# Where eighteen expert-weight slots lie, and when the first fourteen of them may be loaded

## The chip, the cores and the metric

One core of a Trainium2 chip runs the whole program. It has a matrix engine (TensorE, PE in the profile), a vector engine (VectorE, DVE), a scalar engine (ScalarE, ACT), GpSimd (POOL), a queue engine (SyncE, SP) and 16 DMA engines that all queues share. The metric is the device time of one execution in microseconds, the median of several runs.

## The reference

One layer of an encoder trunk on 512 tokens of width 1024, in float32: a token mixer (stick-breaking attention and retention, merged by gates), a cross-attention into 256 memory rows, and a mixture of 32 experts of which each token takes four. After it a final RMSNorm. What the change touches is the seam between the last dense product (`@ w_co`) and the experts:

```python
x = x + memory_cross_attention(rmsnorm(x, g_xattn[l]), rmsnorm(mem, g_mem[l]), w_cq[l], w_ckv[l], w_co[l])
x = x + moe_ffn(rmsnorm(x, g_moe[l]), w_router[l], b_router[l], w_exp_in[l], b_exp_in[l], w_exp_out[l], b_exp_out[l])
...
def expert_block(args):
    xb, e = args
    hc = xb @ w1[e] + b1[e]
    glu = jnp.minimum(hc[..., :D_FF], SWIGLU_LIMIT)
    lin = jnp.clip(hc[..., D_FF:], -SWIGLU_LIMIT, SWIGLU_LIMIT)
    act = glu * jax.nn.sigmoid(SWIGLU_ALPHA * glu) * (lin + 1.0)
    return act @ w2[e] + b2[e]
```

Each expert's `w1` is 1024 x 2048 and its `w2` is 1024 x 1024 values: 12 MB for one expert, 384 MB for all.

## The kernel before

**The dense half.** Twenty-seven slabs of weights (`SLABS`), 52 chunks of 1 MB in all (`DENSE`), go through four `raw` buffers. ScalarE copies each half chunk (a piece, 104 in all, `DP`) into a rounded high part `wh` (`split`, L743), VectorE subtracts to get the low part `wl` (`split`, L1090), and TensorE makes each product of three matmuls (`three`, L1665 to L1667). `wh` and `wl` have six places each; a split of piece g waits until TensorE has used piece g-6. The semaphore `w_lo` counts low parts made, `w_used` counts pieces (and later expert chunks) that TensorE has used. The last slabs are `mv1`, `cq0`, `cq1`, then after the cross-attention `co0` (pieces 96 to 99) and `co1` (100 to 103).

**The expert half.** An expert is 12 chunks of 1 MB: 8 of `w_exp_in`, which `up` uses at L1985, and 4 of `w_exp_out`, which `down` uses at L2009. Chunk k goes to slot k % 18 (`SLOTS`). Twelve slots lie in `ring`, three in `moe`, three in `work`. `ring` and `moe` lie over the dense half's buffers, which are dead by then. In words of one partition, from the start of the overlay: `op2` 0 to 4096, `raw` to 12288, `wh` to 18432, `wl` to 24576, `oph` and `opl` to 32768, `acts`, `bias` and `bsel` to 37504. So ring slots 0 and 1 lie on `op2`, 2 to 5 on `raw`, 6 to 8 on `wh`, 9 to 11 on `wl`, and `moe` starts on `oph`.

**What sets the order.** All weight loads are issued by SyncE's queue, in one fixed order, chunk 0 first (L506 for the experts). A load waits for what still uses the memory of its slot. Slot 0 waits for the last product that reads `op2`; slots 2 to 5 each wait for a low part (`w_lo`), that is for a `raw` buffer to be free; slot 6 waits for `w_used` = 104, the end of `co1`; slot 13 waits for the expert biases to be out of `moe`; slots 15 and 17 wait for steps of the routing. From chunk 18 on a load waits until TensorE has used the chunk 18 before it (`refill`).

**The seam.** When the cross-attention is done, GpSimd issues the small loads of the expert half through its own software queue (L614 to L624): the router's weights, the gains, constants, and three times the expert biases (`bias_f`, 32 rows of 8 KB and 32 rows of 4 KB each). When the biases have landed, GpSimd adds one to a part (L627), then ScalarE and VectorE take turns splitting them into bfloat16 parts (L923, L1309, five steps). Only behind these, in ScalarE's order, stand the squares for the norm (L931) and the copies of the transposed tiles (`router_tile`, L938), for which TensorE waits in the middle of `co1` (`router_product`, L1902).

```python
for s in range(SLOTS):
    if s == 0:
        sp.wait_ge(w_used, 2 * (slabs["mv1"].chunk0 + slabs["mv1"].chunks))
    elif 2 <= s < 6:
        sp.wait_ge(w_lo, 2 * (DENSE - RAW + s - 1))
    elif s == 6:
        sp.wait_ge(w_used, DP)
...
project("co1", op_h, op_l, meanwhile={1: lambda: router_transposes(0), 2: lambda: router_product(0)})
```

Of the kernel before, what the change touches and what calls it, by code (L numbers as in the profile page):

```python
# [15 lines left out]
ALU = mybir.AluOpType  # L16
# [7 lines left out]
P = 128  # L24
# [155 lines left out]
def layer_kernel(nc, x, mem, g_mix, w_in, w_sb_o, w_ret_o, w_mix_out, g_xattn, g_mem, w_cq, w_ckv, w_co,  # L180
# [11 lines left out]
    with ExitStack() as ctx:  # L192
# [11 lines left out]

        ident = sb("ident", [P, P])[:, :]
        small = sb("small", [P, 100])
        work = sb("work", [P, 15360])
        ps = ctx.enter_context(nc.psum_tensor("ps", [P, 8, 512], F32))

# [11 lines left out]


        ring = sb("ring", [P, EC, CH])
        moe = sb("moe", [P, 8192 + 3 * D])
        bias_f = moe[:, 8192:8192 + 3 * D]
        bias_b = sb("bias_b", [P, 2 * D + D], BF16)
        sel_c = sb("sel_c", [P, 3, 32], BF16)

# [59 lines left out]
        sel_b = w_(15232, 64).bitcast(BF16).rearrange("p (t e) -> p t e", t=TT)  # L288
        g_moe_c = small[:, 0:8]
        logit_t = work[:, 6656:7168]  # L290
        square = w_(0, 4096).rearrange("p (t n) -> p t n", t=8)
        ss_more = xmax
        at = 12928
        names = {}
# [6 lines left out]
            names[name] = w_(at, n)  # L301
            at += n
        assert at <= 15104
        w_rt = view(6144, KT, NE)
        top = names["top"].rearrange("p (t n) -> p t n", t=TT)
        topi = names["topi"].bitcast(U32).rearrange("p (t n) -> p t n", t=TT)
        idxf = names["idxf"].rearrange("p (t n) -> p t n", t=TT)
# [39 lines left out]
        sel_now, sel_old, sel_last = (sel_c[0:96, n, :] for n in range(3))  # L347

        def held(s):
            if s < FIRST:  # L350
                return ring[:, s, :] if s < EC else m_(5120 + CH * (s - EC), CH)
            return w_((4096, 6144, 2048)[s - FIRST], CH)

        pick_l = w_(1536, T).rearrange("p (t h n) -> p t h n", t=TT, h=2)
# [1 line left out]
        y_last = m_(5632, 512)  # L356
        junk = m_(0, D)
        pick_30 = w_(0, TT * GR * P).rearrange("p (t j s n) -> p t j s n", t=TT, j=GR, s=4)
        gate_30 = m_(9216, GR * T).rearrange("p (j n) -> p j n", j=GR)
        y_30 = m_(6144, GR * 256).rearrange("p (j n) -> p j n", j=GR)  # L360
        gate_d = [names["oh"][:, P * k:P * k + P] for k in range(TOPK)]
        y_rows = [w_(0, D), w_(D, D)] + [ring[:, s, D * a:D * a + D] for s in range(6, 12) for a in range(2)] + [
            m_(7168, D), m_(8192, D)]
        g_fin_b = w_(5120, D)
        o_sb = view(0, TT, D)

# [53 lines left out]
        def dense_source(g):  # L420

            for s in slabs.values():
                if s.chunk0 <= g < s.chunk0 + s.chunks:
                    break
            half, name = g - s.chunk0, s.name
            order = list(slabs)
            if order.index(name) < 13:
                src, col = w_in[0], order.index(name)
            else:
                src = {"so": w_sb_o, "ro": w_ret_o, "mo": w_mix_out, "mk": w_ckv, "mv": w_ckv,  # L430
                       "cq": w_cq, "co": w_co}[name[:2]][0]
                col = int(name[2]) + (2 if name[:2] == "mv" else 0)
            return src[half * 512:(half + 1) * 512, col * 512:(col + 1) * 512].rearrange("(a p) n -> p a n", p=P)

        def landed_early(slot):
            return 0 if slot < FIRST else 16 * len(range(slot - FIRST, DENSE, RAW))
# [58 lines left out]
        @block.sync  # L495
        def _(sp):
            for t in range(TT):
                sp.dma_start(x_nat[:, t, :], x[0, t * P:(t + 1) * P, :]).then_inc(in_x[t], 16)
            for g in range(DENSE):
                if g >= RAW:  # L500
                    sp.wait_ge(w_lo, 2 * (g - RAW + 1))
                sp.dma_start(raw[:, g % RAW, :].rearrange("p (a n) -> p a n", a=4),
                             dense_source(g)).then_inc(w_landed[g % RAW], 16)

            def load(e, c, s):
                sp.dma_start(held(s), expert_chunk(e, c)).then_inc(w_ring[s], 16)  # L506

            for s in range(SLOTS):
                if s == 0:
                    sp.wait_ge(w_used, 2 * (slabs["mv1"].chunk0 + slabs["mv1"].chunks))  # L510
                elif 2 <= s < 6:
                    sp.wait_ge(w_lo, 2 * (DENSE - RAW + s - 1))
                elif s == 6:
                    sp.wait_ge(w_used, DP)
                elif s == EC + 1:
                    sp.wait_ge(b_hi, 3)
                    sp.wait_ge(b_lo, 2)
                elif s == FIRST:
                    sp.wait_ge(nat_ready, TT)
                    sp.wait_ge(lg_done, 1)  # L520
                elif s == FIRST + 2:
                    sp.wait_ge(h_stored, 16 * TT)
                    sp.wait_ge(xt_made, 1)
                if s < 2 * W1:
                    load(s // W1, s % W1, s)
                else:
                    load(0, W1 + s - 2 * W1, s)

            def expert_at(n):
                return sp.value_load(order[0:1, bass.ds(n, 1)], min_val=0, max_val=NE - 1)  # L530
# [24 lines left out]
            for tt in range(TT):  # L555
                sp.wait_ge(f_last, tt + 1)
                sp.dma_start(out[0, tt * P:(tt + 1) * P, :], o_sb[:, tt, :]).then_inc(stored[tt % 2], 16)
            with sp.If(n > 0):
                sp.wait_ge(row_used, (TT - 1) * TOPK)
                with sp.Fori(0, OVER) as j:  # L560
                    with sp.If(j < n):
                        b = sp.value_load(table[0:1, bass.ds(j, 1)], min_val=0, max_val=OB - 1)
                        sp.wait_ge(w_used, j * EC + (DP + NE * EC))
                        for c in range(EC):
                            load(b % NE, c, c)
                sp.wait_ge(stored[0], 32)
                sp.wait_ge(stored[1], 32)
                for tt in range(TT):
                    sp.wait_ge(f_last, TT + tt + 1)
                    sp.dma_start(out[0, tt * P:(tt + 1) * P, :], o_sb[:, tt, :]).then_inc(stored[tt % 2], 16)  # L570
                sp.wait_ge(stored[0], 64)
                sp.wait_ge(stored[1], 64)
            sp.wait_ge(stored[0], 32)
            sp.wait_ge(stored[1], 32)
# [157 lines left out]
        def _(act):  # L732
            chain = Chain(act, act_chain)

            def split(g):

                slot = g % SPL
                c = g // 2
                if g % 2 == 0:
                    act.wait_ge(w_landed[c % RAW], 16 * (c // RAW + 1))  # L740
                if g >= SPL:
                    act.wait_ge(w_used, g - SPL + 1)
                nc.scalar.activation(wh[:, slot, :], raw[:, c % RAW, g % 2 * PC:(g % 2 + 1) * PC], ACT.Copy).then_inc(w_hi, 1)  # L743

            def take(name, f, meanwhile={}):

# [180 lines left out]
            def squares(half):  # L927
                acc = (ss, ss_more)[half]
                for t in range(TT):
                    act.wait_ge(tile_out["dve"], slabs[f"co{half}"].out0 + t + 1)  # L930
                    nc.scalar.activation(square[:, 4 * half + t, :], res[:, t, half * 512:(half + 1) * 512], ACT.Square,  # L931
                                         accum_out=acc[:, t:t + 1]).then_inc(n_sq, 1)

            def router_tile(k):
# [148 lines left out]
        def _(dve):  # L1083
            chain = Chain(dve, dve_chain)

            def split(g):

                dve.wait_ge(w_hi, g + 1)
                slot = g % SPL
                nc.vector.tensor_tensor(wl[:, slot, :], raw[:, g // 2 % RAW, g % 2 * PC:(g % 2 + 1) * PC], wh[:, slot, :], ALU.subtract).then_inc(w_lo, 1)  # L1090

            def take(name, f, meanwhile={}):
                s = slabs[name]
# [568 lines left out]
        def _(pe):  # L1662
# [6 lines left out]
            def project(name, oh_, ol_, ready=None, meanwhile={}, free={}):  # L1669

                s = slabs[name]
                for c in range(2 * s.chunks):
                    g = 2 * s.chunk0 + c
                    pe.wait_ge(w_lo, g + 1)
                    w_h, w_l = (v[:, g % SPL, :].rearrange("p (a n) -> p a n", a=2) for v in (wh, wl))
                    for t in range(s.tiles):
                        if c == 0 and s.bank_free[t]:
                            owner, count = s.bank_free[t]
# [470 lines left out]
OFF = {3: 0, 2: 128, 1: 384, 0: 768}  # L2149
OFFA = {0: 0, 1: 512, 2: 896, 3: 1152}  # L2150
ROUTER_BANK = (4, 5, 6, 7, 5, 6, 7, 0)
TR_RET = 2 * KT
_S, _N, _O = lay_slabs()
MIXED = _S["mo1"].out0 + 4
# [21 lines left out]
```

## Time and profile before

| what | value |
|---|---|
| runs | 1798.94 us median of 3 (1796.73 to 1800.96) |
| span of the profiled execution | 1794.9 us |
| PE busy | 1712.9 us (95%) |
| DVE, ACT, POOL busy | 464.5, 387.8, 101.7 us |
| dense half and cross-attention | 0 to about 713 us |
| routing, the end of which is the first expert's product | to 738.9 us |
| experts | 738.9 to about 1753 us |
| last rows, norm, store | to 1794.9 us |
| chain that ended last | PE 67%, SP's queue 18%, DMA 6%, DVE 3%, ACT 2% |

The profiled execution spans 1794.9 us, 4.0 us under the median of the runs; sums below are made on the span and 4.0 us is added. The busy share of PE is high everywhere, so it tells little of what ends last: in the expert half the DMA engines are full too, at about 405 GB/s. A wait of SyncE's queue for PE is not idle time of the DMA engines, since other loads stand in the queue meanwhile.

### The profile page before, as it was taken

To read this page: it belongs to the slowest core of one execution; us is meant where nothing else is said; L and a number is where in the kernel's file an instruction comes from. 1 tells how busy PE (TensorE), PEld (TensorE's weight loads), DVE (VectorE), ACT (ScalarE), POOL (GpSimd) and SP (SyncE) were. 2 spreads that over 40 slices of the span, in tenths; PEclk is the share of its full clock that TensorE was granted. 3 is DMA by queue.
4 is the path that set the end of the run, shared out by engine and by line. 5 is a ranking of instruction groups with operands and counts; after the bars stand their busy time and mean duration, and the time that the engine had idled before them with its cause. 6 is when DMAs were issued, how large, how long until landed. Compare 5 with 4: busy or idle time off the path is not lost.

```text
span 1794.9 us, 36459 instructions
## 1 busy us (share of the span) xinstructions
PE 1712.9 (95%) x15742; PEld 955.8 (53%) x15742; DVE 464.5 (26%) x868; ACT 387.8 (22%) x604; POOL 101.7 (6%) x183
## 2 busy tenths in 40 slices
PE   7989999999999999799999999999999999999986
PEld 5766687788788867433434343434334333343333
DVE  4354525423635253571000000000000000010015
ACT  5464232323325334100101000000000000000011
POOL 0011000000000011010000000000000000000012
PEclk9999999999999999899999999999999999999998
DMA  7202221224225313999999999999999999999995
GB/s 240 71 24 83 77 94 62 74 94 164 71 94 188 141 46 86 408 391 407 388 411 399 410 399 411 403 406 406 404 410 400 410 411 401 410 411 401 410 418 226
DMA packets 104736, 500.67 MB, mean 279 GB/s; under 512 B 11062, under 2 KB 21446, under 8 KB 55344
## 3 DMA queue, kind: packets, MB, share of 16 engines
q1 hardware_dynamic: 83904, 461.40, 65.1%
q0 software_dynamic: 7824, 24.33, 4.3%
q10 hardware_dynamic: 12864, 12.72, 2.0%
q8 instruction: 126, 2.06, 0.5%
q14 instruction: 18, 0.15, 0.0%
HBM read 486.31 MB, written 14.81 MB: 279 GB/s over the span
## 4 chain that ended last, share of the span: by engine, by line
PE 67%; SPq 18%; DMA 6%; DVE 3%; ACT 2%; issue 2%; POOL 1%; another core or an unknown queue 0%; ACTq 0%; DVEq 0%
PE ps L1985 19%; SPq L506 17%; PE ps L2009 10%; PE ps L1665 9%; PE ps L1666 9%; PE ps L1667 9%; DMA work<-in_w_exp_in 3%; DMA ring<-in_w_exp_in 2%; PE ps L1762 1%; PE ps L1817 1%; PE ps L1836 1%; PE ps L1943 1%; PE ps L488 1%; PE ps L1976 1%; PE ps L1953 1%
## 5 line engine op out<-in xcount | busy, mean ns | idle before, releaser
L1985 PE MATMUL ps<-ring,moe 128*32 128x512 f32 x3808 | 416.7, 593 | 2.2 <-DMA ring<-in_w_exp_in 1.9
L1985 PEld LDWEIGHTS ps<-ring,moe 128*32 128x32 f32 x3808 | 115.0, 110 | 289.6 <-issue 255.6
L1560 DVE TENSOR_SCALAR moe<-ps 128x768 f32<-128x768 f32 (+1 forms) x32 | 28.0, 875 | 846.7 <-PE ps L1985 846.7
L2009 PE MATMUL ps<-ring,moe 128*32 128x256 f32 x3648 | 202.9, 379 | 0.5 <-DMA ring<-in_w_exp_out 0.5
L1090 DVE TENSOR_TENSOR wl<-raw,wh 128x1024 fp32r<-128x1024 f32 x104 | 126.2, 1224 | 260.4 <-ACT wh L743 260.4
L743 ACT ACTIVATE wh<-raw 128x1024 fp32r<-128x1024 f32 x104 | 109.1, 1059 | 256.6 <-PE ps L1667 256.0
L2009 PEld LDWEIGHTS ps<-ring,moe 128*32 128x32 f32 x3648 | 110.9, 110 | 83.2 <-DMA ring<-in_w_exp_out 1.5
L1665 PE MATMUL ps<-oph,wh 128*128 128x512 f32 x384 | 151.0, 393 | 2.4 <-DVE work L1223 1.6
L1666 PE MATMUL ps<-opl,wh 128*128 128x512 f32 x384 | 149.8, 390 | 0.0
L1667 PE MATMUL ps<-oph,wl 128*128 128x512 f32 x384 | 149.7, 390 | 0.0
L983 ACT ACTIVATE moe<-ps 128x768 f32<-128x768 f32 (+1 forms) x32 | 23.8, 745 | 582.2 <-DVE moe L1560 582.2
L1665 PE MATMUL ps<-wh,oph 128*128 128x512 f32 x288 | 114.5, 397 | 3.8 <-DVE opl L1261 3.0
L1666 PE MATMUL ps<-wl,oph 128*128 128x512 f32 x288 | 112.9, 392 | 0.0
L1667 PE MATMUL ps<-wh,opl 128*128 128x512 f32 x288 | 112.6, 391 | 0.0
L1985 PE MATMUL ps<-work,moe 128*32 128x512 f32 x904 | 102.5, 594 | 5.0 <-DMA work<-in_w_exp_in 5.0
L1985 PE MATMUL ps<-moe 128*32 128x512 f32 x792 | 90.9, 594 | 11.8 <-DMA moe<-in_w_exp_in 11.8
L1665 PEld LDWEIGHTS ps<-oph,wh 128*128 128x128 f32 x384 | 72.5, 189 | 19.4 <-issue 3.6
L1667 PEld LDWEIGHTS ps<-oph,wl 128*128 128x128 f32 x384 | 72.2, 188 | 15.2
L1666 PEld LDWEIGHTS ps<-opl,wh 128*128 128x128 f32 x384 | 72.3, 188 | 14.5
L1985 PEld LDWEIGHTS ps<-work,moe 128*32 128x32 f32 x904 | 26.2, 110 | 79.3 <-issue 56.5
L648 POOL CAST sel_c<-work 96x32 bf16 (+1 forms) x64 | 15.2, 263 | 908.1 <-DVE moe L1372 858.7
L1665 PEld LDWEIGHTS ps<-wh,oph 128*128 128x128 f32 x288 | 54.4, 189 | 17.5 <-issue 4.7
(328 smaller groups left out, 1693.7 us busy)
## 6 DMA issues: line engine op xcount, KB each, us to landing
ring<-in_w_exp_in SPq DMA_DIRECT2D x172, 1024.0 KB, 27.9
ring<-in_w_exp_out SPq DMA_DIRECT2D x86, 1024.0 KB, 29.0
moe<-in_w_exp_in SPq DMA_DIRECT2D x43, 1024.0 KB
work<-in_w_exp_in SPq DMA_DIRECT2D x41, 1024.0 KB, 27.9
raw<-in_w_in SPq DMA_DIRECT2D x26, 1024.0 KB, 5.1
work<-in_w_exp_out SPq DMA_DIRECT2D x22, 1024.0 KB, 29.1
moe<-in_w_exp_out SPq DMA_DIRECT2D x20, 1024.0 KB
raw<-in_w_ckv SPq DMA_DIRECT2D x8, 1024.0 KB, 5.0
```

The source lines that it names most:

```text
L488: ins = nc.tensor.matmul(ps[:, 6 + dt, :], v_x[:, m, a:a + P], prob_t[:, hd % 2, m * T:(m + 1) * T], start=(m == 0), stop=(m == MT - 1))
L506: sp.dma_start(held(s), expert_chunk(e, c)).then_inc(w_ring[s], 16)
L743: nc.scalar.activation(wh[:, slot, :], raw[:, c % RAW, g % 2 * PC:(g % 2 + 1) * PC], ACT.Copy).then_inc(w_hi, 1)
L983: nc.scalar.activation(glu_s[:, 0:g], ps[:, 0:g, 0:256].rearrange("p j (n a) -> p j a n", a=2), ACT.Silu, scale=ALPHA).then_inc(s_ready, 1)
L1090: nc.vector.tensor_tensor(wl[:, slot, :], raw[:, g // 2 % RAW, g % 2 * PC:(g % 2 + 1) * PC], wh[:, slot, :], ALU.subtract).then_inc(w_lo, 1)
L1560: nc.vector.tensor_scalar(act_n[:, 0:g], ps[:, 0:g, 256:512].rearrange("p j (n a) -> p j a n", a=2), 1.0 - LIMIT, 1.0 + LIMIT, ALU.max, AL ...
L1665: nc.tensor.matmul(o, a_hi_, b_hi_, start=start, stop=False)
L1666: nc.tensor.matmul(o, a_hi_, b_lo_, start=False, stop=False)
L1667: return nc.tensor.matmul(o, a_lo_, b_hi_, start=False, stop=stop)
L1762: ins = nc.tensor.matmul(ps[:, 2 * (u % RING) + hh, P * (b - kb):P * (b - kb) + n], neg_from_r if b == kb else neg_ones_r, part, start=Fal ...
L1985: ins = nc.tensor.matmul(ps[32 * s:32 * s + 32, j, :], xt[:, k, 32 * j:32 * j + 32], w[:, s, :, :], start=False, stop=(k == KT - 1), tile_ ...
L2009: ins = nc.tensor.matmul(y_bank(s, j), at[:, a, j, q, :], w[:, a, s, :], start=False, stop=(q == W2 - 1 and a == 1), tile_position=(0, 32 ...
```

## The change

- The two last pieces of the dense half (102 and 103) no longer go to `wh` and `wl` but to a new buffer `wend` of 4096 words, which lies over the start of `work`. Their splits on ScalarE then wait for no use of an older piece. `half_hi` and `half_lo` choose the buffer.
- The slots get another place (`HELD_RING`, `HELD_MOE`): slots 2 and 3 lie at the end of `moe` (over `acts` and `bias`), 4 to 7 on `raw`, and each pair 8/9, 10/11, 12/13 takes one slot on `wh` and one on `wl`. Slot 14 lies in `moe` over `opl`.
- The waits follow: slots 2 and 3 wait only for the end of the stick-breaking attention (`zc_done`), 4 to 7 for the `w_lo` for which 2 to 5 waited, 8, 10, 12 and 14 for `w_used` = 98, 100, 102 and 104.
- `bias_f` moves from `moe` to `work`, and slot 13's wait for it goes. The scratch of the norm's squares (`square`) becomes one place of 512 words instead of eight, so each square waits for the one before it (`n_sq`), and the first for the last step of the biases (`b_hi`).
- `moe` grows from 11264 to 12288 words, and to make room the memory kept for descriptors of GpSimd's software queue goes from its default to 8192 bytes of a partition. `gate_30`, two of the row buffers of the last step and `w_rt` move too.

```diff
+        with nc.sbuf_tensor("wend", [P, 4, PC], F32R) as wend_:
+            wend = wend_
...
-        moe = sb("moe", [P, 8192 + 3 * D])
-        bias_f = moe[:, 8192:8192 + 3 * D]
+        moe = sb("moe", [P, 8192 + 2 * CH])
+        bias_f = work[:, 4096:4096 + 3 * D]
...
-        square = w_(0, 4096).rearrange("p (t n) -> p t n", t=8)
+        square = w_(6144, 512)
...
         def held(s):
+            if s in HELD_MOE:
+                return m_(HELD_MOE[s], CH)
             if s < FIRST:
-                return ring[:, s, :] if s < EC else m_(5120 + CH * (s - EC), CH)
+                return ring[:, HELD_RING[s], :]
             return w_((4096, 6144, 2048)[s - FIRST], CH)
...
+        def half_hi(g):
+            return wend[:, g - (DP - 2), :] if g >= DP - 2 else wh[:, g % SPL, :]
...
-                elif 2 <= s < 6:
-                    sp.wait_ge(w_lo, 2 * (DENSE - RAW + s - 1))
-                elif s == 6:
-                    sp.wait_ge(w_used, DP)
-                elif s == EC + 1:
-                    sp.wait_ge(b_hi, 3)
-                    sp.wait_ge(b_lo, 2)
+                elif s == 2:
+                    sp.wait_ge(zc_done, len(UNITS))
+                elif 4 <= s < 8:
+                    sp.wait_ge(w_lo, 2 * (DENSE - RAW + s - 3))
+                elif s in (8, 10, 12, 14):
+                    sp.wait_ge(w_used, DP - 14 + s)
...
-                if g >= SPL:
+                if SPL <= g < DP - 2:
                     act.wait_ge(w_used, g - SPL + 1)
...
+                    if half or t:
+                        act.wait_ge(n_sq, 10 + 4 * half + t)
+                    else:
+                        act.wait_ge(b_hi, 3)
...
+HELD_RING = {0: 0, 1: 1, 4: 2, 5: 3, 6: 4, 7: 5, 8: 6, 9: 9, 10: 7, 11: 10, 12: 8, 13: 11}
+HELD_MOE = {2: 8192, 3: 8192 + CH, 14: 5120}
...
-    nc = _bacc.Bacc("TRN2", target_bir_lowering=False, num_devices=1)
+    nc = _bacc.Bacc("TRN2", target_bir_lowering=False, num_devices=1, dynamic_dma_scratch_size=8192)
```

SyncE's queue at the seam, the first loads of expert weights. Before:

```order
L506 DMA ring<-in_w_exp_in 128x2048 [waits w_used]
L506 DMA ring<-in_w_exp_in 128x2048
L506 DMA ring<-in_w_exp_in 128x2048 [waits w_lo] x4
L506 DMA ring<-in_w_exp_in 128x2048 [waits w_used]
L506 DMA ring<-in_w_exp_in 128x2048 x5
L506 DMA moe<-in_w_exp_in 128x2048
L506 DMA moe<-in_w_exp_in 128x2048 [waits b_lo,b_hi]
L506 DMA moe<-in_w_exp_in 128x2048
```

And of the change (the line of `load` is now L515):

```order
L515 DMA ring<-in_w_exp_in 128x2048 [waits w_used]
L515 DMA ring<-in_w_exp_in 128x2048
L515 DMA moe<-in_w_exp_in 128x2048 [waits zc_done]
L515 DMA moe<-in_w_exp_in 128x2048
L515 DMA ring<-in_w_exp_in 128x2048 [waits w_lo] x4
L515 DMA ring<-in_w_exp_in 128x2048 [waits w_used]
L515 DMA ring<-in_w_exp_in 128x2048
L515 DMA ring<-in_w_exp_in 128x2048 [waits w_used]
L515 DMA ring<-in_w_exp_in 128x2048
L515 DMA ring<-in_w_exp_in 128x2048 [waits w_used]
L515 DMA ring<-in_w_exp_in 128x2048
L515 DMA moe<-in_w_exp_in 128x2048 [waits w_used]
```

Of the first fifteen loads, six could go before the end of `co1`, and now fourteen; the four on `raw` carry chunks 4 to 7 where they carried 2 to 5, and two loads stand behind each half of `co0` and `co1`.

ScalarE from the last splits to the first squares. Before:

```order
L743 ACTIVATE wh<-raw 128x1024 [waits w_used]
L743 ACTIVATE wh<-raw 128x1024 [waits w_used,w_landed3]
L743 ACTIVATE wh<-raw 128x1024 [waits w_used]
L923 ACTIVATE bias_b<-moe 96x3072 [waits b_one]
L923 ACTIVATE bias_b<-moe 64x3072 [waits b_lo]
L923 ACTIVATE bias_b<-moe 32x3072 [waits b_lo]
L924 ACT_TABLE_LOAD
L931 ACTIVATE work,small<-work 128x512 [waits tile_out_dve] x4
L938 ACTIVATE work<-ps 128x512 [waits ht_done] x4
```

And of the change:

```order
L750 ACTIVATE wh<-raw 128x1024 [waits w_used]
L750 ACTIVATE wend<-raw 128x1024 [waits w_landed3]
L750 ACTIVATE wend<-raw 128x1024
L930 ACTIVATE bias_b<-work 96x3072 [waits b_one]
L930 ACTIVATE bias_b<-work 64x3072 [waits b_lo]
L930 ACTIVATE bias_b<-work 32x3072 [waits b_lo]
L931 ACT_TABLE_LOAD
L942 ACTIVATE work,small<-work 128x512 [waits b_hi,tile_out_dve]
L942 ACTIVATE work,small<-work 128x512 [waits n_sq,tile_out_dve] x3
L949 ACTIVATE work<-ps 128x512 [waits ht_done] x4
```

Nothing changes its place on ScalarE; the two last splits lose their wait for TensorE, and the squares gain one each.

## Rows read from the trace of the kernel before

**Rows 1.** Timeline of SP's queue (start us, us, engine, line, operation, count).

```profile
597.21 0.98 SPq L506 DMA_DIRECT2D ring<-in_w_exp_in  x2
...
666.44 0.33 SPq L506 DMA_DIRECT2D ring<-in_w_exp_in  x1
...
676.86 0.33 SPq L506 DMA_DIRECT2D ring<-in_w_exp_in  x1
...
712.79 3.06 SPq L506 DMA_DIRECT2D ring<-in_w_exp_in  x6
...
741.55 2.90 SPq L506 DMA_DIRECT2D ring<-in_w_exp_out  x2
```

**Rows 2.** DMA of SP's queue, 713 to 1734, then 712 to 741 (packets, MB, share).

```profile
q1 hardware_dynamic: 53644, 390.71, 94.6%
...
q1 hardware_dynamic: 1215, 8.91, 75.7%
```

**Rows 3.** Chain that ended last (start us, us, what): the biases, routing, last chunk.

```profile
670.49 11.52 DMA moe<-in_b_exp_out
682.09 2.80 POOL moe L627
...
701.35 2.57 ACT work L931 x8
...
727.45 9.73 PE ps L2094 x64
...
738.90 20.66 PE ps L1985 x192
...
1703.65 29.97 DMA work<-in_w_exp_in
```

**Rows 4.** Longest wait of TensorE for weights after 739 (us in total, times, longest).

```profile
PE ps L1985 <- DMA moe<-in_w_exp_in: 11.8, 16, 1.0
```

**Rows 5.** Issue to landing of 1 MB (last number, us): lone; at 840; at 1250.

```profile
raw<-in_w_co SPq DMA_DIRECT2D x4, 1024.0 KB, 5.0
...
work<-in_w_exp_out SPq DMA_DIRECT2D x1, 1024.0 KB, 7.8
...
ring<-in_w_exp_out SPq DMA_DIRECT2D x2, 1024.0 KB, 33.1
```

**Rows 6.** Timeline of TensorE where it waits in `co1`.

```profile
706.00 1.06 PE L1902 MATMUL ps<-work 128*32 128x512 f32 x8 [2.57 <-ACT work L938]
```

**Rows 7.** DMA by queue, 664 to 682, then 667.5 to 670.5; q0 is GpSimd's.

```profile
q0 software_dynamic: 656, 2.12, 55.0%
q1 hardware_dynamic: 261, 1.98, 34.5%
...
q1 hardware_dynamic: 109, 0.89, 85.2%
q0 software_dynamic: 20, 0.02, 10.3%
```

**Rows 8.** Timeline of ScalarE: the splits of pieces 102 and 103.

```profile
669.12 1.06 ACT L743 ACTIVATE wh<-raw 128x1024 fp32r<-128x1024 f32 x1 [3.96 <-PE ps L1667]
674.50 1.06 ACT L743 ACTIVATE wh<-raw 128x1024 fp32r<-128x1024 f32 x1 [4.32 <-PE ps L1667]
```

**Rows 9.** Windows of PE: us, busy (matmuls), granted clock, DMA share, GB/s.

```profile
703.50:706.00 2.50, 0.00 (x0) 1.00 0.00 0
...
728.00:731.00 3.00, 3.00 (x16) 0.50 1.00 418
733.00:736.00 3.00, 3.00 (x30) 1.00 1.04 436
```

**Rows 10.** Timeline of ScalarE: squares that wait for each other, then squares that don't.

```profile
535.69 0.19 ACT L767 ACTIVATION_READ_ACCUMULATOR ps<-work 128x1 f32 x1
535.91 1.03 ACT L767 ACTIVATE ps<-work 128x1024 f32<-128x1024 f32 x1
...
701.89 0.19 ACT L931 ACTIVATION_READ_ACCUMULATOR work<-work 128x1 f32 x1
701.99 0.62 ACT L931 ACTIVATE work<-work 128x512 f32<-128x512 f32 x1
```

More of the change, by code:

```diff
@@ L303, in layer_kernel @@
         assert at <= 15104
-        w_rt = view(6144, KT, NE)
+        w_rt = names["oh"][:, 0:KT * NE].rearrange("p (k e) -> p k e", k=KT)
         top = names["top"].rearrange("p (t n) -> p t n", t=TT)
@@ L358, in layer_kernel @@
         pick_30 = w_(0, TT * GR * P).rearrange("p (t j s n) -> p t j s n", t=TT, j=GR, s=4)
-        gate_30 = m_(9216, GR * T).rearrange("p (j n) -> p j n", j=GR)
+        gate_30 = ring[:, 11, 0:GR * T].rearrange("p (j n) -> p j n", j=GR)
         y_30 = m_(6144, GR * 256).rearrange("p (j n) -> p j n", j=GR)
         gate_d = [names["oh"][:, P * k:P * k + P] for k in range(TOPK)]
-        y_rows = [w_(0, D), w_(D, D)] + [ring[:, s, D * a:D * a + D] for s in range(6, 12) for a in range(2)] + [
-            m_(7168, D), m_(8192, D)]
+        y_rows = [w_(0, D), w_(D, D)] + [ring[:, s, D * a:D * a + D] for s in range(4, 11) for a in range(2)]
         g_fin_b = w_(5120, D)
@@ L433, in dense_source, with half_lo @@
             return src[half * 512:(half + 1) * 512, col * 512:(col + 1) * 512].rearrange("(a p) n -> p a n", p=P)
+        def half_hi(g):
+            return wend[:, g - (DP - 2), :] if g >= DP - 2 else wh[:, g % SPL, :]
+        def half_lo(g):
+            return wend[:, 2 + g - (DP - 2), :] if g >= DP - 2 else wl[:, g % SPL, :]
         def landed_early(slot):
@@ L735, in split @@
             def split(g):
-                slot = g % SPL
                 c = g // 2
@@ L740, in split @@
                     act.wait_ge(w_landed[c % RAW], 16 * (c // RAW + 1))
-                if g >= SPL:
+                if SPL <= g < DP - 2:
                     act.wait_ge(w_used, g - SPL + 1)
-                nc.scalar.activation(wh[:, slot, :], raw[:, c % RAW, g % 2 * PC:(g % 2 + 1) * PC], ACT.Copy).then_inc(w_hi, 1)
+                nc.scalar.activation(half_hi(g), raw[:, c % RAW, g % 2 * PC:(g % 2 + 1) * PC], ACT.Copy).then_inc(w_hi, 1)
             def take(name, f, meanwhile={}):
@@ L930, in squares @@
                     act.wait_ge(tile_out["dve"], slabs[f"co{half}"].out0 + t + 1)
-                    nc.scalar.activation(square[:, 4 * half + t, :], res[:, t, half * 512:(half + 1) * 512], ACT.Square,
+                    if half or t:
+                        act.wait_ge(n_sq, 10 + 4 * half + t)
+                    else:
+                        act.wait_ge(b_hi, 3)
+                    nc.scalar.activation(square, res[:, t, half * 512:(half + 1) * 512], ACT.Square,
                                          accum_out=acc[:, t:t + 1]).then_inc(n_sq, 1)
@@ L1088, in split @@
                 dve.wait_ge(w_hi, g + 1)
-                slot = g % SPL
-                nc.vector.tensor_tensor(wl[:, slot, :], raw[:, g // 2 % RAW, g % 2 * PC:(g % 2 + 1) * PC], wh[:, slot, :], ALU.subtract).then_inc(w_lo, 1)
+                nc.vector.tensor_tensor(half_lo(g), raw[:, g // 2 % RAW, g % 2 * PC:(g % 2 + 1) * PC], half_hi(g), ALU.subtract).then_inc(w_lo, 1)
             def take(name, f, meanwhile={}):
@@ L1674, in project @@
                     pe.wait_ge(w_lo, g + 1)
-                    w_h, w_l = (v[:, g % SPL, :].rearrange("p (a n) -> p a n", a=2) for v in (wh, wl))
+                    w_h, w_l = (v.rearrange("p (a n) -> p a n", a=2) for v in (half_hi(g), half_lo(g)))
                     for t in range(s.tiles):
```

## Prediction

> **What bounds the kernel now.** I read the profile in this order: the DMA engines by queue, then SyncE's queue, then the chain that ended last, then the waits of TensorE. The question for each is what the expert half runs at and from when.
>
> From 713 to 1734 us SyncE's queue moved 390.71 MB and took 94.6% of the sixteen engines [rows 2]; with the other queues nothing is left. That is 1021 / 390.71 x 1.049 = 2.74 us for a chunk of 1 MB (1.049 million bytes), side traffic included. The last of the chain in the experts is such a chunk at 1703.65 [rows 3], and TensorE's largest wait after 739 us is for chunks too, 11.8 us in 16 waits [rows 4]. So the expert half ends when the stream of chunks ends, and TensorE follows it. Before 713 us the engines stand idle: 0 GB/s at 703.5 to 706 [rows 9]. The stream starts with the load behind `w_used` = 104, at 712.79 [rows 1].
>
> Taken alone this promises much for a change that loads eight more chunks before 713. But two more things have to be read. The first is the slots. A chunk beyond the eighteenth waits until TensorE has used one, and the first use starts with the first expert's product at 738.90 [rows 3]; the first refill is issued at 741.55 [rows 1]. The second is how much backlog the queue has later. A lone chunk lands 5.0 us after its issue; at 1250 us it takes 33.1 us, since loads stand ahead of it, but at 840 us only 7.8 us [rows 5]. There the stream is held nearly at TensorE's pace: 7.8 - 5.0 = 2.8 us of transfers stand in the queue, and no more. From there on it runs full to the end.
>
> The seam from 670 to 739 us is a chain of its own. The biases land, GpSimd starts at 682.09, the squares at 701.35 [rows 3], and TensorE has waited 2.57 us in the middle of `co1` when it goes on at 706.00 [rows 6]. What makes the biases later makes the first expert later, one for one.
>
> **Part by part: the earlier loads.** By 741 us the queue has moved 8.91 MB since 712 us [rows 2], 8.5 chunks, and with the six from before some 14.5 are there. With the change fourteen are in before the end of `co1`, and the last four follow before the first use, so 18 are. That is a lead of 3.5 chunks, 3.5 x 2.74 = 9.6 us. It can't be kept. With all slots full the stream goes at TensorE's pace through the first experts, and what it can win against the kernel before is the backlog at the tightest place, 2.8 us. Its bounds: zero, if a load beside the small transfers of that stretch takes 7.8 us anyway; 9.6 us, if the landing time at 840 us were no sign of a backlog. I take 2.8, from the rows that measure it there.
>
> **Part by part: the price at the seam.** Once the lead is capped, the stream hangs on TensorE: every microsecond by which the first expert starts later is one at the end. Three things delay it.
>
> First, the biases. From 664 to 682 us GpSimd's queue takes 55.0% of the engines, 9.9 us of work, and SyncE's 34.5%, 6.2 us for its two chunks (issued at 666.44 and 676.86 [rows 1]), 3.1 us each [rows 7]. They don't share evenly: while the first chunk was moved, 667.5 to 670.5, SyncE's queue had 85.2% and GpSimd's 10.3% [rows 7]. Now there are four chunks in that time instead of two. The one on the third `raw` buffer still goes at 666.44. The fourth followed the split of piece 103, which waited for TensorE until 674.50 [rows 8]; without the waits the two splits run right behind each other, and the load goes at about 669. Chunks 8 and 9 wait for `w_used` = 98, the very event that released the split at 674.50. Chunks 10 and 11 come two pieces later; a piece takes 674.50 - 669.12 = 5.4 us [rows 8], so 685.3.
>
> GpSimd's queue had some 1.5 us of its work done by 667.5, and 8.4 us left. Data follows an issue after about 1.2 us. Chunks 6 and 7 hold the engines from 667.5 to 673.8; GpSimd's queue gets a tenth, 0.6 us. Alone to 675.8: 2.0. Chunks 8 and 9 to 682.0: 0.6. Alone to 686.5: 4.5. That is 7.7 of the 8.4 us when chunks 10 and 11 begin, so it is a close thing: either the rest slips through, or it waits for two more chunks. In the kernel before the data was through by about 679, and GpSimd started 3.1 us later, with a chunk in between. I take the first: through at 686.6, a start at 689.7, 7.6 us later than 682.09. The bounds: nothing, if the two queues overlap; 13.5 us, if the last rows wait for chunks 10 and 11 (2 x 3.1 us more, less a little).
>
> A rule speaks on this. The Trainium skill, DMA: Bandwidth & Descriptors, section Queues, rings and completion order, says that each DMA engine goes round the queues that have work, a packet from each in turn. The row disagrees at first sight, 85.2% to 10.3% [rows 7]. What an even share would give is the third rival below.
>
> Second, the squares. Four stand in the chain; three now wait for the one before. With such waits the next starts 0.22 us after the read of the accumulator, without them 0.10 us [rows 10]: 3 x 0.12 = 0.4 us. The four later ones wait for VectorE anyway.
>
> Third, the clock of TensorE. A pause of 2.5 us left it at 1.00 [rows 9]. Now the pause is 2.57 + 7.6 + 0.4 = 10.6 us. After the pause ahead of 727.45 [rows 3] the granted clock was 0.50 (1.2 GHz), with 16 matmuls in 3 us where 30 fit at 1.00 [rows 9], and it came back between 731 and 733. That is about 4 us at half speed, so 2.0 us lost; between 0 and 2.8.
>
> **What costs nothing.** Slots 2 and 3 at 597.21 [rows 1] go behind the last dense load, and GpSimd's queue is empty there. Slot 13's wait for the biases was over before its turn at 712.8. The moves of `bias_f`, `w_rt`, `gate_30` and the row buffers change addresses, not instructions. The smaller memory for descriptors could make GpSimd stop among its twelve small loads; no row shows such a stop, and it would add to the first term; I take zero.
>
> **The sum.** 7.6 + 0.4 + 2.0 = 10.0 us by which the first expert starts later, less 2.8 us of backlog: 7.2 us. On the span, 1794.9 + 7.2 = 1802.1; with 4.0 us between span and median, 1806.1 us, 0.4% slower.
>
> **The rivals.**
>
> A, forecast: biases 7.6 us late, 1806.1 us. Chance 0.42.
>
> B, the biases miss the gap and wait for chunks 10 and 11: 13.5 + 0.4 + 2.0 - 2.8 = 13.1, so 1812.0 us. For it: the working above comes out 0.7 us short. Against it: at the ends of a chunk both queues move at once. Chance 0.12.
>
> C, an even share of the queues: the 8.4 us take 16.8 us from 667.5, to 684.3, 5.3 us after 679. 5.3 + 0.4 + 2.0 - 2.8 = 4.9, so 1803.8 us. That is what the Trainium skill's rule on turns would give, and [rows 7] speaks against it. Chance 0.13.
>
> D, the biases are hardly later. They are bound by their 32 rows in few partitions, not by the engines, and the chunks pass beside them. Then 0 to 2 us + 0.4 - 2.8, between -2.4 and -0.4: about 1797.5 us, no clock loss. For it: 2.12 MB took 9.9 us of work, half the rate of a weight chunk. Against it: the 10.3%. Chance 0.20.
>
> E, faster: the lead counts in full. If the 7.8 us at 840 us are not a backlog of 2.8 but the landing time of a stream that was never held, the end moves by the whole 9.6 us, less the 0.4: 1789.7 us. It decides from the point where the queue would run empty between 741 and 860 us; if it never does, E holds. Against it: SyncE's refills go out in TensorE's rhythm from 741.55 on [rows 1], and the landing time is lowest there and grows after [rows 5]. With a late first expert E would give about 1800. Chance 0.13.
>
> **How the numbers follow.** Slower by over 0.2% (3.6 us, about what the measurement of this kernel can tell from no change) are A, B and C: 0.67. Within 0.2% is D: 0.20. Faster is E: 0.13. The range from 1796.5 to 1813.0 us takes in A to D with their bounds and leaves E out.
>
> **What would show it.** In the profile after: fourteen loads issued before the end of `co1`; GpSimd's add on the biases at about 690 instead of 682.09 (rivals: 696, 687, 683); TensorE's pause before the router's product near 10 us, and a clock of 0.50 after it; the first expert's product at about 749; DMA engines idle between some 735 and 750; landing times of 5 to 6 us up to 860; the last chunk in the chain landing 7 us later than 1733.6. The forecast is wrong if GpSimd's add comes before 685, or if loads keep a landing time well over 8 us through the first four experts.

## The result, and the profile after

| | before | after |
|---|---|---|
| median of 16 runs each | 1796.45 us | 1801.72 us |
| ratio | | 1.0032 (95% interval 1.0021 to 1.0042) |
| span of the profiled execution | 1794.9 us | 1798.6 us |
| forecast | | 1806.1 us (1796.5 to 1813.0), slower 0.67 |

The changed kernel is 5.3 us slower, 0.32%. The forecast was 7.2 us, 0.40%. The forecast time is 4.4 us above the measured one: 1.9 us of it lie in the forecast difference, and 2.5 us in its base, a median of three runs (1798.94 us) where 16 runs gave 1796.45.

First the queue that the change moves. SyncE's queue in the kernel after (start us, us, line, operation, count; one row from each of five stretches):

```profile
606.32 88.94 SPq L515 DMA_DIRECT2D ring<-in_w_exp_in  x10
...
666.86 0.33 SPq L515 DMA_DIRECT2D ring<-in_w_exp_in  x1
...
672.68 0.80 SPq L515 DMA_DIRECT2D ring<-in_w_exp_in  x2
...
683.56 0.80 SPq L515 DMA_DIRECT2D ring<-in_w_exp_in  x2
...
718.97 0.33 SPq L515 DMA_DIRECT2D moe<-in_w_exp_in  x1
```

The change does what it says: chunks 0 to 13 are issued by 695.3 (606.32 + 88.94), only chunk 14 waits for the end of `co1`. What matters more stands in the rows between. Chunk 7 goes at 666.86, right behind chunk 6 (664.59), where the kernel before issued its second chunk of this stretch at 676.86 [rows 1]; chunks 8 and 9 follow at 672.68.

Now the seam, which is the chain of [rows 3, 6]. GpSimd in the kernel before and then after, its first small load and its add on the biases:

```profile
663.87 0.75 POOL L614 DMA_DIRECT2D work<-in_c_mats  x1 [232.78 <-PE ps L488]
```

```profile
662.02 0.75 POOL L622 DMA_DIRECT2D work<-in_c_mats  x1 [231.09 <-PE ps L497]
...
685.08 2.79 POOL L635 TENSOR_SCALAR work<-work 96x1024 f32<-96x1024 f32 x1 [15.94 <-DMA work<-in_b_exp_out]
```

All of this execution lies 1.85 us earlier, 662.02 against 663.87, before anything of the change has run; in the twelve traces of the experiments this point lies between 661.9 and 664.7 us with no order among the kernels. So I count from the first small load: the add comes after 18.2 us before (682.09 [rows 3]) and after 23.1 us now. With the 1.85 us added, chunks 6 to 9 were issued at 666.4, 668.7 and 674.5, as forecast.

TensorE in the kernel after, where it waits in `co1`, its windows there (us, busy, granted clock, DMA share, GB/s), and the chain at the first expert and at the last chunk:

```profile
709.59 1.94 PE L1912 MATMUL ps<-work 128*32 128x512 f32 x8 [7.97 <-ACT work L949]
```

```profile
704.00:709.00 5.00, 0.00 (x0) 0.59 0.00 0
710.00:714.00 4.00, 4.00 (x14) 0.50 0.00 0
716.00:719.00 3.00, 3.00 (x16) 1.00 0.00 0
...
735.00:744.00 9.00, 8.88 (x67) 0.78 0.00 0
```

```profile
745.29 2.08 PE ps L1995 x17
...
1708.47 29.98 DMA work<-in_w_exp_in
```

The pause is 7.97 us where it was 2.57 [rows 6]. The granted clock falls to 0.50 (1.2 GHz) within it; after it 14 matmuls take 4 us, where 16 take 3 us once the clock is back. The eight short matmuls of the router take 1.94 us instead of 1.06.

And the DMA engines between the end of `co1` and the first refill. From 712 to 741 us SyncE's queue moved 8.91 MB at 75.7% before [rows 2]; after, from 713 to 741:

```profile
q1 hardware_dynamic: 432, 3.15, 30.3%
```

With the other queues the engines are busy for half of this stretch; the last window above, 735 to 744 us, has 0 GB/s. The weights are there, and nothing may be loaded over them yet.

### The profile page after: what moved, and what is told of

It is laid out like the page before. It is cut to its first block, busy times and chain, and to the rows that moved or that the text cites. A ratio compares the mean times of both kernels' runs of the same rounds, so it can differ in the third digit from the quotient of the medians.

```text
span 1798.6 us, 36465 instructions
## 1 busy us (share of the span) xinstructions
PE 1711.9 (95%) x15742; PEld 955.5 (53%) x15742; DVE 464.2 (26%) x868; ACT 387.4 (22%) x604; POOL 101.4 (6%) x183
## 4 chain that ended last, share of the span: by engine, by line
PE 67%; SPq 17%; DMA 6%; issue 3%; DVE 3%; ACT 2%; POOL 1%; another core or an unknown queue 0%; ACTq 0%; DVEq 0%; POOLq 0%
PE ps L1995 19%; SPq L515 16%; PE ps L2019 10%; PE ps L1675 9%; PE ps L1676 9%; PE ps L1677 9%; DMA work<-in_w_exp_in 5%; PE ps L1772 1%; PE ps L1827 1%; PE ps L1846 1%; DMA work<-in_b_exp_out 1%; PE ps L1953 1%; PE ps L1986 1%; PE ps L497 1%; PE ps L1963 1%
## 5 line engine op out<-in xcount | busy, mean ns | idle before, releaser
L1995 PE MATMUL ps<-ring,moe 128*32 128x512 f32 x3168 | 350.6, 594 | 11.0 <-DMA ring<-in_w_exp_in 11.0
L2019 PE MATMUL ps<-ring,moe 128*32 128x256 f32 x4320 | 239.6, 379 | 1.5 <-DMA ring<-in_w_exp_out 1.5
L1995 PE MATMUL ps<-moe 128*32 128x512 f32 x1432 | 161.2, 592 | 3.5 <-DMA moe<-in_w_exp_in 3.5
L1675 PE MATMUL ps<-wh,oph 128*128 128x512 f32 x272 | 107.3, 395 | 3.8 <-DVE opl L1271 3.0
L1676 PE MATMUL ps<-wl,oph 128*128 128x512 f32 x272 | 105.9, 389 | 0.0
L1677 PE MATMUL ps<-wh,opl 128*128 128x512 f32 x272 | 105.9, 389 | 0.0
L1995 PEld LDWEIGHTS ps<-moe 128*32 128x32 f32 x1432 | 43.1, 110 | 106.8 <-issue 88.7
```

Of the source, the lines that this page charges most:

```text
L1675: nc.tensor.matmul(o, a_hi_, b_hi_, start=start, stop=False)
L1676: nc.tensor.matmul(o, a_hi_, b_lo_, start=False, stop=False)
L1677: return nc.tensor.matmul(o, a_lo_, b_hi_, start=False, stop=stop)
L1995: ins = nc.tensor.matmul(ps[32 * s:32 * s + 32, j, :], xt[:, k, 32 * j:32 * j + 32], w[:, s, :, :], start=False, stop=(k == KT - 1), tile_ ...
L2019: ins = nc.tensor.matmul(y_bank(s, j), at[:, a, j, q, :], w[:, a, s, :], start=False, stop=(q == W2 - 1 and a == 1), tile_position=(0, 32 ...
```

## The sum, measured

Counted in spans of the two profiled executions:

| stretch | before | after | difference |
|---|---|---|---|
| start to the first small load | 663.87 | 662.02 | -1.85 |
| first small load to the first expert's product | 75.03 | 83.27 | +8.24 |
| of it: GpSimd's add later | 18.22 | 23.06 | +4.84 |
| of it: from the add to the router's product | 23.91 | 24.51 | +0.60 |
| of it: from the router's product to the first expert | 32.90 | 35.70 | +2.80 |
| first expert to the landing of the last chunk | 994.72 | 993.16 | -1.56 |
| last chunk to the end | 61.28 | 60.15 | -1.13 |
| span | 1794.9 | 1798.6 | +3.7 |

Without the first line, which no part of the change touches, it is 5.5 us, and the medians say 5.3.

Each column is one execution, and the two small gains in it, 1.56 and 1.13 us, are not seen again. In the traces of another chip (after_again, and before_small, which is the kernel before but for its descriptor memory; both below) the stretch from the first small load to the first expert's product grows by 7.9 us, and from there to the end it takes 1050.5 us with the change and 1050.4 us without. The means of the runs of these two kernels are 7.7 us apart (2.4 us either way). What made the end shorter by 1.13 us here stays open.

## Experiments

Each ratio is to runs of the kernel before on the same chip; the kernel before took 1788.5 to 1791.0 us there. The chips differ, so I compare ratios, and traces by the time from the first small load. Each kernel has one trace. hold6, hold8, before_hold and after_early ran on one chip, before_small, after_again, before_early and after_early2 on a second, the other four on a third.

**Hold the weights until the biases have landed (hold6).** One wait more in the changed kernel:

```diff
                 elif 4 <= s < 8:
+                    if s == 6:
+                        sp.wait_ge(in_bias, 96)
```

> The changed kernel with one wait more: SyncE's queue holds chunk 6 and all behind it until the biases have landed. My theory (the price at the seam is the transfers of weights beside the biases): the biases land with no weights beside them, so GpSimd's add comes about 13 us after its first small load is issued instead of 23.1 us (18.2 us before the change), TensorE's pause before the router's product (8.0 us, 2.6 us before the change) goes, the clock stays at 1.00 there, and the first expert starts 2.6 us earlier against the seam than before the change. With 1.6 us of lead the time is about 4 us under the kernel before, ratio 0.9977. Rival (the price lies in the smaller descriptor memory or in the other addresses): GpSimd's add stays late and the ratio stays at 1.003.

Measured: 1.0002 (0.9993 to 1.0012). The trace of this kernel, GpSimd, ScalarE's second bias step, VectorE's last tile of `co0` and its first bias step, TensorE:

```profile
661.88 0.75 POOL L624 DMA_DIRECT2D work<-in_c_mats  x1 [231.09 <-PE ps L497]
675.33 2.79 POOL L637 TENSOR_SCALAR work<-work 96x1024 f32<-96x1024 f32 x1 [6.36 <-DMA work<-in_b_exp_out]
...
683.42 0.69 DVE L1315 TENSOR_TENSOR work<-ps,work 128x512 f32<-128x512 f32 x1 [0.67 <-PE ps L1679]
684.03 3.34 DVE L1321 TENSOR_TENSOR work<-work,bias_b 64x3072 f32<-64x3072 f32 x1
...
702.92 1.06 PE L1914 MATMUL ps<-work 128*32 128x512 f32 x8 [1.45 <-ACT work L951]
```

The add comes after 13.5 us, as expected, and the whole loss of the change is gone. But the gain beyond that, expected at 0.9977, is missing. The biases are ready on ScalarE at 681, and VectorE takes its first step of them only at 684.03, right behind its last tile of `co0`. The steps stand behind those tiles in VectorE's order. So biases that land early win nothing: the chain has a floor, and the pause of 1.45 us is this floor plus the squares.

**Hold only chunks 8 and 9 (hold8).**

```diff
                 elif s in (8, 10, 12, 14):
+                    if s == 8:
+                        sp.wait_ge(in_bias, 96)
```

> The changed kernel, where only chunk 8 and what is behind it wait for the biases; chunks 6 and 7 go beside them as in the changed kernel. My theory: as many chunks beside the biases as before the change, so GpSimd's add comes 17 to 18 us after the first small load is issued, the pause of TensorE is 2 to 3.2 us, no clock loss, and the lead of 1.6 us is left: ratio about 0.999. If chunks 8 and 9 had no part in the delay, the add stays near 23 us and the ratio at 1.003.

Measured: 1.0024 (1.0013 to 1.0036), and this expectation was wrong. The trace:

```profile
664.71 0.75 POOL L624 DMA_DIRECT2D work<-in_c_mats  x1 [232.56 <-PE ps L497]
684.21 2.79 POOL L637 TENSOR_SCALAR work<-work 96x1024 f32<-96x1024 f32 x1 [12.38 <-DMA work<-in_b_exp_out]
...
708.72 1.94 PE L1914 MATMUL ps<-work 128*32 128x512 f32 x8 [4.41 <-ACT work L951]
```

With as many chunks beside the biases as in the kernel before the add still comes only after 19.5 us, the pause is 4.41 us, and the eight matmuls after it again take 1.94 us: the clock has fallen. Chunks 8 and 9 are not the main cause. hold6 on the same chip shows that the weights from chunk 6 on are: with them held too the ratio was 1.0002, and the means are 4.8 us apart (1.9 us either way). What is left in hold8, beside the moved buffers, is that chunk 7 goes right behind chunk 6.

**The kernel before with held weights (before_hold).** Chunks 4 and 5 wait for `in_bias` as in hold6.

> The kernel before, with chunks 4 and 5 held until the biases have landed. My theory says that the kernel before pays for its two chunks too: GpSimd's add about 13 us after the first small load instead of 18.2 us, TensorE's pause of 2.6 us gone, all behind it 2.6 us earlier, ratio 0.9986. If two chunks are hidden and only four are too many: ratio 1.000.

Measured: 1.0007 (0.9998 to 1.0017). GpSimd's add comes after 13.3 us, and the pause is still 0.84 us, since VectorE's first bias step starts at 685.24, behind its tile of `co0` at 684.63. The floor again. On these chips the kernel before pays nearly nothing for its two chunks.

**Only the descriptor memory (before_small).** The kernel before with `dynamic_dma_scratch_size=8192`.

> The kernel before, with only the descriptor memory of GpSimd's queue set to 8192 bytes of a partition, as in the changed kernel (all buffers lie 8192 bytes lower with it). My theory: no part of the loss, ratio 1.000, GpSimd's twelve small loads issued in the same 6.6 us. Rival: GpSimd stops for descriptors, ratio 1.001 to 1.003.

Measured: 0.9991 (0.998 to 1.0002): no part of the loss. Its trace also is the mark for the kernel before on such a chip:

```profile
663.06 0.75 POOL L614 DMA_DIRECT2D work<-in_c_mats  x1 [231.16 <-PE ps L488]
679.61 2.79 POOL L627 TENSOR_SCALAR moe<-moe 96x1024 f32<-96x1024 f32 x1 [9.44 <-DMA moe<-in_b_exp_out]
```

Here the add comes after 16.55 us, not 18.2, and the pause is 0.86 us: nearly at the floor. Each is one trace, and the changed kernel differs as much between two of its own (23.1 us, and 20.8 in after_again). So times of the add from different chips compare to some 2 us only; whether the chip or the execution makes that, no run shows.

**Chunk 7 at its old time (hold7).** The changed kernel with hold8's wait and one more:

```diff
                 elif 4 <= s < 8:
+                    if s == 7:
+                        sp.wait_ge(w_used, DP - 6)
```

> The changed kernel with chunk 7 issued only after the piece (w_used = 98) at which the kernel before issued its second chunk beside the biases, and chunk 8 and all behind it after the biases. Theory now: with chunk 8 and 9 held alone, GpSimd's add stayed 19.5 us after the first small load, so it is the earlier chunk 7 (about 669 instead of 675 to 677 us, since the last splits have lost their wait) that delays the biases most. Then here the add comes at 16.5 to 18 us, TensorE's pause is 1.5 to 2.6 us, the clock stays at 1.00 and the ratio is 1.000 to 1.001. Rival: two chunks beside the biases delay them by as much wherever they start; then the add stays at 19.5 us and the ratio at 1.002.

Measured: 0.9993 (0.998 to 1.0006).

```profile
664.31 0.75 POOL L626 DMA_DIRECT2D work<-in_c_mats  x1 [232.44 <-PE ps L497]
680.56 2.79 POOL L639 TENSOR_SCALAR work<-work 96x1024 f32<-96x1024 f32 x1 [9.17 <-DMA work<-in_b_exp_out]
...
705.36 1.07 PE L1916 MATMUL ps<-work 128*32 128x512 f32 x8 [1.45 <-ACT work L953]
```

Between hold8 and hold7 one load is issued 5.8 us later (10.66 us after the first small load, not 4.84; in the kernel before it was 12.99), so that it starts 8.1 us behind chunk 6 and not 2.3. The add goes from 19.5 back to 16.25 us, the pause from 4.41 to 1.45 us, and the ratio from 1.0024 to 0.9993, though on another chip. hold7 keeps all of the change's moved buffers and the squares' waits, so these cost nothing that can be measured.

**Only the free splits (before_wend).** The kernel before with `wend` and the one-place scratch for the squares, and nothing else. No load is added.

```diff
-                if g >= SPL:
+                if SPL <= g < DP - 2:
                     act.wait_ge(w_used, g - SPL + 1)
```

> The kernel before with only the buffer wend for the two last pieces (and the one-place scratch of the squares that makes room for it, with its waits). Slots, biases and all other waits are as before, so no load is added; only chunk 5 can go at about 669 instead of 675 to 677 us. Theory: that alone brings GpSimd's add to 19.5 us after the first small load, a pause over 4 us, the clock at 0.50 after it, and a ratio of about 1.003, as the whole change. Rival (the added chunks 8 and 9 are the cause): add at 16.5 to 18 us, ratio 1.000 to 1.001, from the squares' 0.6 us.

Measured: 1.0013 (1.0001 to 1.0024). Chunk 5 goes early, the add comes after 18.7 us, the pause is 3.65 us, and the clock falls:

```profile
707.17 1.93 PE L1910 MATMUL ps<-work 128*32 128x512 f32 x8 [3.65 <-ACT work L947]
```

```profile
704.00:706.00 2.00, 0.00 (x0) 1.00 0.00 0
706.00:708.00 2.00, 0.83 (x5) 0.73 0.00 0
708.00:710.00 2.00, 2.00 (x10) 0.50 0.00 0
```

So a buffer that frees two splits costs by itself, with the chunks added nowhere. The plainest comparison is with hold7 on the same chip, which also has two chunks beside the biases, but 8.1 us apart: add after 16.25 us against 18.7, ratio 0.9993 against 1.0013, a difference of 3.4 us in the means that is clear of the noise of these runs (1.4 us either way). The expected 1.003 was missed: it is not the whole loss, 1.0013 against the 1.0031 of the changed kernel. One reason can be read from the traces: the clock was back at 1.00 by 712 us here and only after 715 us in the changed kernel, and from the router's product to the first expert it took 1.0 us more than in the first trace of before, where the changed kernel took 2.8 more. In time to the add the parts line up, across three chips: 16.55 us (before_small), 18.7 and 19.5 us (chunk 5 or 7 early: before_wend, hold8), 20.8 us (after_again). No run has chunks 8 and 9 early and chunk 7 at its old time.

**The changed kernel again (after_again).**

> The changed kernel itself on the same chip, as the mark for the others: 1.003.

Measured: 1.0031 (1.0018 to 1.0045), as in the first comparison. The add comes at 684.40, after 20.8 us, and the pause is 5.76 us.

**Biases out of the seam (after_early, after_early2, before_early).** Their loads go behind the stick-breaking attention, into the words of `acts`, and the five steps beside the slabs `gs0` to `gr0`. The core of the edit, on ScalarE:

```diff
                 take(f"gs{n}", into)
+                bias_part(n)
...
                 take(f"gr{n}", into)
+                if n == 0:
+                    bias_part(2)
...
-            act.wait_ge(b_one, 1)
-            for part in range(3):
-                if part:
-                    act.wait_ge(b_lo, part)
```

> The changed kernel, with the biases loaded into the end of moe right after the stick-breaking attention and split beside the retention's gates, long before the seam; chunks 2 and 3 wait for that. Nothing but small constants is then loaded by GpSimd at the seam, and ScalarE has no bias steps there. My theory: no pause of TensorE before the router's product, the first expert 2.6 us earlier against the seam than before the change, lead 1.6 to 2.8 us: 4 to 5 us under the kernel before, ratio about 0.9975. The rival on the lead (it counts in full, 9.6 us, once the seam doesn't hold it back): ratio 0.993.

> The kernel before with the early biases alone (loaded after the stick-breaking attention, split beside the retention's gates); slots and waits as before. My theory: TensorE's pause of 2.6 us goes, the first expert 2.6 us earlier, ratio 0.9986. Against the changed kernel with early biases it tells what the earlier fill is worth by itself: 1.6 to 2.8 us if the lead is capped by the slots, 9.6 us if not.

> The changed kernel with early biases again, on the same chip as the kernel before with early biases, for the difference between the two: 1.6 to 2.8 us less if the lead is capped, about 9.6 us less if it counts in full.

Measured: after_early 1.0005 (0.9994 to 1.0016). On another chip, the other two together: before_early 0.9981 (0.9973 to 0.999), after_early2 0.9986 (0.9977 to 0.9995). The pause is gone in all three:

```profile
704.10 1.06 PE L1904 MATMUL ps<-work 128*32 128x512 f32 x8
```

(before_early; the row has no idle time before it). The first expert comes 72.9 us after the first small load there, 73.5 in before_small on the same chip, 75.0 in the first trace of before. Two things follow. Biases out of the seam take the whole loss of the change away; whether they gain beyond the kernel before is 0.2% on one chip and not seen on the other. And the earlier fill is worth nothing that can be measured: 0.9986 with it, 0.9981 without it, on the same chip; the means are 0.3 us apart, 1.4 us either way, so a gain of a microsecond isn't excluded. The expected 0.9975 of after_early was missed. The lead in full would have been 9.6 us, 0.5%.

**Where the lead counts (lead_as_before, lead_less).** Both are after_early with a wait more: in the first, chunk 6 and all behind it wait for the end of `co1` (the old lead in the new slots), in the second chunk 0 does.

> The changed kernel with early biases (0.9986 to 1.0005 of the kernel before in two measurements), in which chunk 6 and all behind it wait for the end of co1, as in the kernel before: the place of the slots is new, the lead is the old one. If the lead is capped by the slots, the loss against early biases with the new lead is 0 to 2 us: ratio 0.998 to 1.001. If the lead counted in full it would be 9.6 us slower: 1.004.

> The changed kernel with early biases, in which no expert chunk at all is loaded before the end of co1: the stream starts six chunks or 16.4 us later than in the kernel before. It tells from which lead on the stream hangs on TensorE. With a backlog of 1 to 2.8 us at the tightest place in the kernel before, 13.6 to 15.4 us of it should show: ratio 1.007 to 1.0085. If the lead before were already much more than enough, it would cost little: below 1.003.

Measured: 0.999 (0.9979 to 1.0001) and 1.0064 (1.0048 to 1.008). Issue to landing of 1 MB chunks (last number, us): from 830 to 850 us lead_as_before, then from 850 to 866 us lead_less:

```profile
ring<-in_w_exp_out SPq DMA_DIRECT2D x2, 1024.0 KB, 7.1
```

```profile
ring<-in_w_exp_in SPq DMA_DIRECT2D x4, 1024.0 KB, 22.1
```

The old lead is enough. With six chunks less the queue has a real backlog all through the first experts, and now the stream's start counts: from the first expert to the end it is 1062.4 us in lead_less against 1051.4 in lead_as_before. Of the 16.4 us by which the stream starts later 11 show. By this count some 5 us of the old lead were already lost; I take it that a queue held short by the slots moves less than a deep one, but no run here shows that apart. That more lead brings nothing is what the early biases measured. lead_less came out below my expectation of 1.007 to 1.0085.

## Why the prediction was right, and where it was not

**What bounds the kernel, and the seam one for one: right.** All of the loss lies between the first small load and the first expert (+8.24 us), and some of it comes back after in this pair (-1.56, and -1.13 that was not forecast), where the forecast said +10.0 and -2.8.

**The earlier loads: the mechanism right, the term too large.** I took 2.8 us, the difference between 7.8 us at 840 us and 5.0 us for a lone load [rows 5]. It measured 1.56 us in the pair of traces and nothing in the comparison of early biases. What failed is the 5.0 us as the floor. In the kernel after the engines do run short of work (SyncE's queue takes 76.9% of them from 770 to 790 us, GpSimd's 6.2%), and still (issue to landing, 830 to 850 us):

```profile
work<-in_w_exp_out SPq DMA_DIRECT2D x1, 1024.0 KB, 6.6
```

A chunk takes 6.4 to 6.9 us from issue to landing in both stretches, not the 5 to 6 us forecast; what keeps it there, gathers and row stores or the chunk ahead of it, no run separates. By these rows 7.8 - 6.6 = 1.2 us would have been the term; on the other chip it is 7.3 (before_small) less 6.9 (after_again), 0.4 us. The bound at zero was set for just this case.

**The biases: right in kind, too large, and with the wrong culprit first.** I took 7.6 us and it measured 4.84 us. The step that failed is the tenth that GpSimd's queue was to get beside weights [rows 7]. Shares of the DMA engines in the kernel after, 665.5 to 668.5 us (chunk 6), then 670 to 674 us (chunk 7):

```profile
q1 hardware_dynamic: 100, 0.82, 83.9%
q0 software_dynamic: 33, 0.04, 16.8%
...
q1 hardware_dynamic: 118, 0.93, 66.7%
q0 software_dynamic: 146, 0.50, 38.4%
```

The first chunk does shut GpSimd's queue out. In hold6, where no weights are under way from 665.5 to 668.5 us, GpSimd's queue has work and gets the engines (its first small load goes 0.14 us before that of the kernel after, so the stretch is the same); in the kernel after, from 675 to 678 us, it keeps them, although chunks 8 and 9 were issued at 672.68 (last row: SyncE's queue from 664 to 678 us):

```profile
q0 software_dynamic: 202, 0.58, 91.3%
...
q0 software_dynamic: 152, 0.66, 101.4%
q1 hardware_dynamic: 11, 0.03, 5.2%
...
q1 hardware_dynamic: 288, 2.10, 44.9%
```

So the tenth holds for chunk 6 only. Beside chunk 7 GpSimd's queue gets 38.4%, and chunks 8 and 9, which the forecast gave the engines from 675.8 on, moved nothing before 678: from 664 to 678 us SyncE's queue moved 2.10 MB, which chunks 6 and 7 make up. Why these two started 5 us after their issue stays open.

The measured 4.84 us lies below even rival C's 5.3 us, and rival C's total of 4.9 us is nearer to the measured 5.3 than my 7.2; I had given it a chance of 0.13 against 0.42. Rival C was the even share that I had drawn from the Trainium skill's rule on turns (DMA: Bandwidth & Descriptors, section Queues, rings and completion order). Counted in packets, the trace agrees with the rule for chunk 7 (118 to 146), but not for chunk 6 (100 to 33, where hold6 shows 202 packets of GpSimd's queue alone).

I had named chunk 7's earlier start but counted the delay from all four chunks alike. Its start right behind chunk 6 makes 2.5 us (before_wend against hold7, one chip) to 3.3 us (hold8 against hold7, two chips). For chunks 8 and 9 there is only a difference across chips: 1.3 us to after_again's 20.8, 3.6 us to the 23.1 of the first trace.

**A floor I had not seen.** "What makes the biases later makes the first expert later, one for one" holds only above the floor that VectorE's tiles of `co0` set. In the trace of before the biases lay above it (VectorE's first step 1.6 us after its last tile), which is why it came out here. hold6 and before_hold, which should have won 2.6 us by it, won nothing.

**The squares:** 0.4 us forecast, 0.60 measured. **The clock:** 2.0 us forecast, 2.8 measured, at the upper bound given. Both too small. These two errors and the lead that was taken too large all made the forecast faster, and the bias term, 2.8 us too large, made it slower. That the sum, 10.0 - 2.8 = 7.2 us, came as near to 5.3 as it did is in part luck.

**What costs nothing: right** for the descriptor memory, 0.9991 (0.998 to 1.0002), and for the moved buffers, as hold7's 0.9993 shows.

**The rivals.** D (no delay) fell by the add at 23.1 us (and its "half the rate" was 0.21 against 0.32 MB per us, two thirds [rows 7]), B by the same (it needed 31.7). C's mechanism holds for one chunk and its numbers came nearer than mine. E fell by the idle DMA engines, 0 GB/s from 735 to 744 us, by lead_as_before, and by after_early2, which is no faster than before_early. My own sign of being wrong, an add before 685, was nearly met: the add came at 685.08 in an execution that lay 1.85 us early, and at 684.40 in after_again, whose first small load lies within 0.3 us of that of before. By that mark alone after_again would speak against the forecast, and it lost the same 0.31%.

## What to carry to other kernels

A prefetch is worth only what the queue lacks at its tightest later place; here eight chunks more brought nothing that could be measured, while six less cost 11 us. What a wait held back may have been a spacing that something else lived on: freeing two splits sent a load right behind another, into the few microseconds in which small loads of the critical chain were under way. Before a load is moved earlier, look at what lands in that stretch, and at which instructions set the floor of that chain.

## What the runs showed of the hardware that I had not expected

- A 1 MB load from SyncE's queue left GpSimd's queue 10% (before) and 17% (after) of the DMA engines over three microseconds, where it had 91% without that load (hold6); a second load right behind the first left it 38%. Two such loads 2.3 us apart delayed the 1.2 MB of biases by 2.5 us more than two 8.1 us apart (before_wend, hold7).
- The other way round, two such loads issued at 672.68, while the biases were under way in GpSimd's queue, moved nothing before 678 us (kernel after).
- The clock of TensorE stayed at 1.00 through pauses of 0.9, 1.45 and 2.6 us and fell to 0.50 in pauses of 3.65, 4.4, 5.8 and 8.0 us. After the longest it cost 2.8 us up to the first expert, after the shortest of these 1.0 us.
